# Retention's value and gate projection, and half of its query and key projection in layer two, as three products of parts

## The reference

```
mod = silu(c) @ w_ada[l] + b_ada[l]                 # shift, scale and gate, six times 1024
h = x * (1 + sc_m) + sh_m
(aq, ak, av, iq, ik, iw, rq, rk, rv, rg, mq, mk, mv, mo, mi, mf) = split(h @ w_in[l])   # 1024 x 3916
o_a = attention(rope(aq), rope(ak), av), the 64 best keys chosen by an index of iq, ik, iw
o_b = head_norm(retention(rope(rq), rope(rk), rv)) * silu(rg)
o_c = head_norm(sigmoid(mo) * mlstm(silu(conv(mq, mk)), mv, mi, mf))
x = layer_norm(ALPHA * x + (1 + g_m) * (concat(o_a, o_b, o_c) @ w_out[l]))
h = x * (1 + sc_f) + sh_f
x = layer_norm(ALPHA * x + (1 + g_f) * experts(h))   # 16 experts, 2 of them weighted per token
```

## Time and profile before

| | us |
|---|---|
| median of 3 runs | 1697.02 |
| lowest and highest of them | 1693.13, 1697.38 |
| the profiled execution's own time | 1697.81 |
| its span, first to last instruction | 1696.0 |
| TensorE, VectorE, ScalarE busy | 1634.5, 1082.3, 716.0 |

### The profile page before, as it was taken

How to read it: one execution, slowest core, us unless ns; L and a number is a source line. 1 busy time by engine, 2 the same in 40 slices (tenths; PEclk the granted TensorE clock), 3 DMA queues, 4 the chain that set the end, 5 groups by cost and what they waited for, 6 DMA issues and landing times.

```text
span 1696.0 us, 19169 instructions
## 1 busy us (share of the span) xinstructions
PE 1634.5 (96%) x7463; PEld 1244.0 (73%) x7463; DVE 1082.3 (64%) x1684; ACT 716.0 (42%) x1105; POOL 0.2 (0%) x4
## 2 busy tenths in 40 slices
PE   6999999999999999999999989899999998999998
PEld 5465568888885655688888878778887887788885
DVE  8678587776656765884545567864546767754445
ACT  1133343433421333433434346653436756643445
POOL 0000000000000000000000000000000000000000
PEclk9998999999999999999999999899999998999999
DMA  9856356877764633556555652146556451444641
GB/s 353 296 182 242 122 186 223 316 254 273 248 230 161 229 110 108 187 198 220 177 187 185 217 167 99 49 149 204 169 200 222 145 187 50 149 149 164 208 170 41
DMA packets 218538, 314.98 MB, mean 186 GB/s; under 512 B 22468, under 2 KB 147788, under 8 KB 218320
## 3 DMA queue, kind: packets, MB, share of 16 engines
q1 hardware_dynamic: 217760, 313.63, 53.6%
q10 hardware_dynamic: 688, 0.13, 0.0%
HBM read 312.70 MB, written 1.05 MB: 185 GB/s over the span
## 4 chain that ended last, share of the span: by engine, by line
PE 85%; DVE 10%; ACT 2%; issue 1%; DMA 1%; SPq 0%; DVEq 0%; ACTq 0%
PE psum L598 18%; PE psum L599 18%; PE psum L600 18%; PE psum L534 8%; PE psum L1008 3%; DVE tmp L1336 2%; PE psum L605 2%; DVE gring_parts L1333 1%; PE psum L1206 1%; PE psum L651 1%; PE psum L517 1%; PE psum L574 1%; PE psum L575 1%; DVE arena L1336 1%; PE psum L1182 1%
## 5 line engine op out<-in xcount | busy, mean ns | idle before, releaser
L600 PE MATMUL psum<-arena_parts,hT_parts 128*128 128x512 f32 x896 | 353.0, 394 | 0.0
L1333 DVE TENSOR_TENSOR gring_parts<-gring,arena_parts 128x2048 fp32r<-128x2048 f32 (+1 forms) x125 | 278.9, 2271 | 50.6 <-ACT arena_parts L2356 50.0
L2356 ACT ACTIVATE arena_parts<-gring 128x2048 fp32r<-128x2048 f32 (+1 forms) x125 | 231.3, 1904 | 0.4
L1333 DVE TENSOR_TENSOR arena_parts<-psum,ex_parts 128x256 fp32r<-128x256 f32 x106 | 44.5, 420 | 281.1 <-ACT ex_parts L2356 280.9
L2356 ACT ACTIVATE ex_parts<-psum 128x256 fp32r<-128x256 f32 x106 | 40.5, 382 | 394.2 <-PE psum L651 394.2
L598 PE MATMUL psum<-arena_parts,o_cat_parts 128*128 128x512 f32 x512 | 203.8, 398 | 0.0
L599 PE MATMUL psum<-gring_parts,o_cat_parts 128*128 128x512 f32 x512 | 202.3, 395 | 0.0
L600 PEld LDWEIGHTS psum<-arena_parts,hT_parts 128*128 128x128 f32 x896 | 168.5, 188 | 39.6
L534 PE MATMUL psum<-gring,hT 128*128 128x512 f32 x384 | 176.1, 609 | 2.5 <-DMA gring<-in_w_in 1.8
L598 PE MATMUL psum<-arena_parts,ex_parts 128*128 128x512 f32 x424 | 177.3, 418 | 0.3 <-DVE arena_parts L1333 0.3
L599 PE MATMUL psum<-gring_parts,arena_parts 128*128 128x512 f32 x432 | 170.3, 394 | 0.0
(11 more groups left out here) (268 smaller groups left out, 2386.5 us busy)
## 6 DMA issues: line engine op xcount, KB each, us to landing
gring<-in_w_ffn_in SPq DMA_DIRECT2D x44, 1024.0 KB, 8.8
gring<-in_w_ada SPq DMA_DIRECT2D x20, 2048.0 KB, 9.8
gring<-in_w_in SPq DMA_DIRECT2D x16, 2048.0 KB, 12.4
gring<-in_w_gate SPq DMA_DIRECT2D x32, 1024.0 KB, 7.4
gring<-in_w_up SPq DMA_DIRECT2D x32, 1024.0 KB, 9.8
dring<-in_w_down SPq DMA_DIRECT2D x32, 1024.0 KB, 5.0
dring<-in_w_ffn_out SPq DMA_DIRECT2D x22, 1024.0 KB, 5.0
gring<-in_w_out SPq DMA_DIRECT2D x8, 2048.0 KB, 8.7
```

The costliest lines, as they stand in the source:

```text
L600: return nc.tensor.matmul(ps, lo, w, start=False, stop=stop)
L1333: return nc.vector.tensor_tensor(o, a, b, op)
L2356: return nc.scalar.activation(o, a, ACT.Copy)
```

## The change

Where in_parts lists a range of k tiles of a chunk, these k tiles become products of parts: in layer one k tiles 0 to 3 and 6, 7 of rvg; in layer two 0 to 3 of rqk and all of rvg. The rounded weights get places that are free at that time: rows, tmp, the upper half of o_cat and parts of the arena. The rounded input (in_hi) and its rest (in_lo) lie in the two slots of dring. ScalarE makes the rounded parts (input_rounded, projection_rounded), VectorE the rests (input_rest, projection_rest). In layer one all this work is at s = 5 on ScalarE and at s = 7 on VectorE. In layer two the input's parts come ahead of the rotations of idx, rqk's behind att_exp(1) and att_in(1), rvg's at s = 5 and s = 7. The row loads move behind the loads of the second expert's gate and up weights, gu1. (blocks, queries and keys, pT_blocks and ex_blocks name places; not all are used.)

```diff
@@ -260,7 +260,7 @@
         cshared = sb("cshared", [P, C_SHARED])
         cblock = sb("cblock", [P, C1_W])
         crows = sb("crows", [NR, NR, P])
-        rows = sb("rows", [P, 2, D])
+        rows, rows_parts = sb_parts("rows", [P, 2, D])
         gb = sb("gb", [P, D])
         ones = sb("ones", [P, SEQ])
         pcol = sb("pcol", [P, 2 * P])
@@ -276,7 +276,7 @@
         hidT = ex_parts[:, 2, :].rearrange("p (t f n) -> p t f n", t=TT, f=FE // P)
         prm = ex[:, 1, 0:2 * P].rearrange("p (a n) -> p a n", a=2)
         small = sb("small", [P, SMALL])
-        tmp = sb("tmp", [P, 2, N])
+        tmp, tmp_parts = sb_parts("tmp", [P, 2, N])
         arena, arena_parts = sb_parts("arena", [P, ARENA])
         ident = cshared[:, 0:P]
         scoresT = tmp[0:NE, 0, 0:SEQ]
@@ -403,6 +403,7 @@
 
         roped = buf(3, N)
         idxT, aqT, akT, rrT = buf(3, SEQ), buf(4, SEQ), buf(4, SEQ), buf(4, SEQ)
+        at_rows = used[0] - SEQ * 4
         av, rvg = buf(TT, N), buf(TT, N)
         rv, rg = rvg[:, :, 0:256], rvg[:, :, 256:512]
         qkT, mo = buf(4, SEQ), buf(TT, 256)
@@ -410,6 +411,21 @@
         score = buf(SEQ)
         sm, pT = buf(2, N), buf(2, N)
         tail = used[0]
+
+        def blocks(at, n):
+
+            return arena_parts[:, at:at + n * N].rearrange("p (k n) -> p k n", n=N)
+
+        in_hi = dring_rest[:, 0].rearrange("p t (k n) -> p t k n", n=P)
+        in_lo = dring_rest[:, 1].rearrange("p t (k n) -> p (t k) n", n=SEQ)
+        first_half, upper = [a.rearrange("p t (k n) -> p (t k) n", n=N) for a in (rows_parts, o_cat_parts)]
+        queries, keys = blocks(at_rows, 8), upper
+        pT_blocks, ex_blocks, heads = blocks(tail - 2 * N, 2), ex_parts[:, 0:2, :], o_cat_parts[:, :, N:D]
+        in_parts = {
+            (0, "rvg"): [(0, 4, first_half), (6, 8, heads)],
+            (1, "rqk"): [(0, 2, blocks(at_rows, 2)), (2, 4, blocks(at_rows + 4 * N, 2))],
+            (1, "rvg"): [(0, 4, first_half), (4, 6, tmp_parts[:, :, :]), (6, 8, heads)],
+        }
         cin, mv = buf(4, SEQ + CONV - 1), buf(TT, NR, HD + 1)
         acc = tmp
 
@@ -533,6 +549,20 @@
             for k in ks:
                 last = nc.tensor.matmul(ps[:, 0:n], hT[:, k, t * P:(t + 1) * P], w[:, k, 0:n],
                                         start=k == 0, stop=k == KT - 1)
+            return last
+
+        def token_parts(ps, l, t, name, ks=range(KT)):
+
+            part_of = {k: (k0, a[:, k - k0, :]) for k0, k1, a in in_parts.get((l, name), ()) for k in range(k0, k1)}
+            n = slice(t * P, (t + 1) * P)
+            for k in ks:
+                if k in part_of:
+                    k0, w = part_of[k]
+                    if t == 0 and k == k0:
+                        pe.wait_ge(vector_done, V.at(T, ("in lo", name, k0)))
+                    last = split_product(ps, in_hi[:, t, k, :], in_lo[:, k, n], w, g_rest(T.stage, name)[:, k, 0:N], k == 0, k == KT - 1)
+                else:
+                    last = nc.tensor.matmul(ps, hT[:, k, n], gslot(T.stage, name)[:, k, 0:N], start=k == 0, stop=k == KT - 1)
             return last
 
         def wait_weights(name, q):
@@ -773,7 +803,7 @@
                 if name == "idx":
                     last = product_as_modulated(ps, t, gslot(stage, name), N_IDX)
                 else:
-                    last = token_product(ps, t, gslot(stage, name), N)
+                    last = token_parts(ps, l, t, name)
                 last.then_inc(tensor_done, T.step((name, t)))
 
             def half_in_proj(name, t, q):
@@ -782,7 +812,7 @@
                     if t == 0:
                         pe.wait_ge(G.sem(stage, name), G.level(stage, name))
                     take((name, t), V if name == "rqk" else A, 6 if (name, t) == ("rqk", 1) else 5)
-                last = token_product(bank(T, (name, t)), t, gslot(stage, name), N, range(4 * q, 4 * q + 4))
+                last = token_parts(bank(T, (name, t)), l, t, name, range(4 * q, 4 * q + 4))
                 if q:
                     last.then_inc(tensor_done, T.step((name, t)))
 
@@ -1645,6 +1675,21 @@
                     normed("in", t)
                 modulated("xT", "hT", 1, scale, shift)
 
+            def input_rest():
+
+                for t in range(TT):
+                    dve.wait_ge(scalar_done, A.at(V, ("in hi", t)))
+                    n = slice(t * P, (t + 1) * P)
+                    for half in range(2):
+                        k = slice(4 * half, 4 * half + 4)
+                        tt(in_lo[:, k, n], hT[:, k, n], in_hi[:, t, k, :], ALU.subtract).then_inc(vector_done, V.step())
+
+            def projection_rest(name):
+
+                for k0, k1, w in in_parts[l, name]:
+                    dve.wait_ge(scalar_done, A.at(V, ("in hi", name, k0)))
+                    tt(g_rest(stage, name)[:, k0:k1, 0:N], gslot(stage, name)[:, k0:k1, 0:N], w, ALU.subtract).then_inc(vector_done, V.step(("in lo", name, k0)))
+
             slots = {}
 
             def rope_chunk(name, t, nh):
@@ -1768,6 +1813,8 @@
                 dve.wait_ge(vector_done, V.now())
 
 
+            if l:
+                input_rest()
             for t in range(TT):
                 if l == 0:
                     rotation_tables(t)
@@ -1785,6 +1832,8 @@
             top_k(1)
             att_in(0)
             att_in(1)
+            if l:
+                projection_rest("rqk")
             for s in range(len(ATT)):
                 if s + 2 < len(ATT):
                     att_in(s + 2)
@@ -1820,6 +1869,9 @@
                         tt(wr_parts[:, :], wr[:, :], wr_hi_parts[:, :], ALU.subtract).then_inc(vector_done, V.step())
                         dve.wait_ge(vector_done, V.now())
                 if s == 7:
+                    if l == 0:
+                        input_rest()
+                    projection_rest("rvg")
                     rope_chunk("rqk", 1, 2 * NR)
                     columns_of(9)
                     if l == 0:
@@ -2465,6 +2517,22 @@
                     root_of("in", rstd[:, t:t + 1], t)
                     modulated_T("xT", "hT", t, *folded["mix"])
 
+            def input_rounded():
+
+                for t in range(TT):
+                    act.wait_ge(vector_done, V.at(A, ("hT", t, 0)))
+                    if l:
+                        act.wait_ge(tensor_done, T.of(FIRST[l - 1], ("dn1", NE - 1)))
+                        act.sem_inc(waited)
+                    act.wait_ge(scalar_done, A.now())
+                    copy(in_hi[:, t, :, :], hT[:, :, t * P:(t + 1) * P]).then_inc(scalar_done, A.step(("in hi", t)))
+
+            def projection_rounded(name, *free):
+
+                act.wait_ge(G.sem(stage, name), G.level(stage, name))
+                for k0, k1, w in in_parts[l, name]:
+                    copy(w, gslot(stage, name)[:, k0:k1, 0:N]).then_inc(scalar_done, A.step(("in hi", name, k0)))
+
             def row_T(name, dst, blocks, t):
                 act.wait_ge(tensor_done, T.at(A, (name, "T", t)))
                 ps = bank(A, (name, "T", t))
@@ -2476,6 +2544,8 @@
                 for t in range(TT):
                     row_T(name, dst, blocks, t)
 
+            if l:
+                input_rounded()
             rows_T("idx", idxT, 3)
 
             def relu(t):
@@ -2546,6 +2616,8 @@
             act.wait_ge(scalar_done, A.now())
             att_exp(0)
             att_exp(1)
+            if l:
+                projection_rounded("rqk")
             copied_mqk(1)
             for s in range(len(ATT)):
                 att_probs_T(s)
@@ -2562,6 +2634,14 @@
                         act.wait_ge(tables_loaded, 16 * TABLES)
                         act.wait_ge(vector_done, V.of("start", "wr_pad"))
                         copy(wr_hi_parts[:, :], wr[:, :]).then_inc(scalar_done, A.step("wr"))
+                if s == 5:
+                    if l == 0:
+                        input_rounded()
+                    else:
+                        act.wait_ge(vector_done, V.at(A, ("affine", "in", 1)))
+                        act.wait_ge(tensor_done, T.at(A, ("sum", "ada5")))
+                        act.sem_inc(waited)
+                    projection_rounded("rvg")
                 if s == 6:
                     act.wait_ge(vector_done, V.at(A, "conv"))
                     activate(qkT, qkT, ACT.Silu).then_inc(scalar_done, A.step("conv"))
@@ -2968,17 +3048,16 @@
                             sp.wait_ge(vector_done, V.at(S, ("read", ("out", 1, h))))
                         sp.sem_inc(waited)
                     load_gate_bias(l, 4)
-                if name == "wo1":
-                    if l:
-                        sp.wait_ge(vector_done, V.at(S, ("affine", "in", 1)))
+
+            def expert(name, e):
+                return by_row(ins[name][l:l + 1, e:e + 1].rearrange("a b c d -> (a b c) d"))
+
+            for e in range(NE):
+                load_halves(stage, f"gu{e}", expert("w_gate", e), expert("w_up", e))
+                if e == 1:
```

(7 more changed lines are left out.)

4 lines of the change are left out of this document (2 added, 2 removed).

## The result

| | median | from .. to | executions |
|---|---|---|---|
| before | 1697.84 us | 1693.02 .. 1698.49 | 9 |
| changed | 1702.45 us | 1699.03 .. 1706.63 | 9 |

The ratio is 1.0031, with a 95% interval of [1.002, 1.0041]: slower by 0.31%, about 5 us. The change was forecast at 1698.8. The time lies inside the range (1692.8 to 1703.0), near its upper end; it is just past 1702.1, where the forecast began to say slower, with a chance of 0.14. The profiled execution of the changed kernel took 1706.61 us (span 1704.8), one of its slowest; its mean granted clock was 0.979, against 0.984 before.

The account below looks back on a forecast made before the run. TensorE, at work for 96% of the span, was taken as the bound. Layer one +1.5, layer two -1.4 and clock +1.7 gave +1.8 on the profiled 1697.81, so 1699.6, or 1698.8 us on the median; range 1692.8 to 1703.0.

Parts of the forecast that it names:

- the clock: Behind the new gap ahead of rvg in layer one, one stretch at 1.2 GHz was counted, costing 1.66 us.
- The second rival: Slower by the clock in both layers: three 1.2 GHz stretches, +5.1 in sum, 1702.1 us; chance 0.15.
- Layer one, VectorE: Six subtractions ahead of the rotation take 6.27 us, only 2.72 of it in idle time; TensorE waits 3.5 (3.2 to 3.9).
- The sum of layer one: Layer one's wait for VectorE less the gain of shorter products: 3.5 - 1.98 = +1.5 us.
- Layer one, ScalarE: The copies behind att_exp(7) take 5.10 us in all and are hidden, with 0.2 to spare.
- Layer two, start: Two copies and four subtractions ahead of the rotations of idx cost 0; were they not hidden, at most 3.6.
- Layer two, mvo: Two copies ahead of the copy of mqk's second block hold up mvo: +0.6 us, bounds 0.4 and 0.7.
- Layer two, the lost gains: rqk's saving of 1.32 and that of rvg's first half end in waits for the Silu and the values.
- The halves: A half_in_proj call with all four k tiles as products of parts saves 0.66 us, one with two changed 0.33.
- The sum without the clock: Both layers' changes with no lower clock behind the new gap: +0.1 us.
- One rival's sum: No gain on TensorE, from equally slow products or late rvg weights: +6 us, 1703; chance 0.02.
- the 1.98 of layer one: Gain of layer one's four halves of rvg as products of parts: 0.66, 0.33, 0.66 and 0.33 us.

Follow-up runs that it names:

- the second trace: The changed kernel executed again with no edit: 1702.44 us, ratio 1.0027 to the kernel before.
- the moved loads: The kernel before with only the two row loads of the layer norm moved behind gu1: 1697.21 us, ratio 0.9995.
- layer two alone: The changed kernel with products of parts, copies and subtractions only in layer two, layer one as before: 1700.39 us, ratio 1.0002 to before.
- layer one filled: The changed kernel with five idle matmuls ahead of rvg in layer one only: 1701.7 us, ratio 1.002 to before.
- room and rqk: Parts for k tiles 4 to 7 of rvg in layer one, rvg and rqk in layer two: 1697.09 us, ratio 0.9993 to before.
- room: The changed kernel with parts only for k tiles 4 to 7 of rvg in layer one, and rvg in layer two: 1692.55 us, ratio 0.997 to before.
- layer one alone: The changed kernel with products of parts, copies and subtractions only in layer one, layer two as before: 1698.83 us, ratio 1.0003 to before.
- the gap alone: The kernel before with row loads moved and six unread VectorE subtractions of the same sizes in layer one, no parts: 1704.81 us, ratio 1.0033.
- layer two filled: The changed kernel with two idle matmuls ahead of mLSTM's first scores in layer two only: 1701.63 us, ratio 1.0016 to before.

## Why the prediction was wrong

**The step that failed is the clock:** "This gap is longer than those, so I count one such stretch", at 1.66. Both the number and the price were too low. Two stretches come in both traces of the changed kernel: behind the gap of layer one, 5.24 - 2.78 = 2.5, and behind the wait for the Silu (634 to 640), 6.22 - 3.70 = 2.5 on rqk alone. Together they are 5.0 where the sum has 1.7, and over the executions the clock's figure is 5.5 more than before, some of it in the gap itself. That is the miss: 1702.4 against 1698.8. The first profile has two more stretches. Whether the one from 172.75 belongs to the change is open: it is missing from the second trace, but both kernels with one gap filled have it (granted clock 0.83 and 0.80 from 170 to 180). The one at 650 can't be put down to the change: a stretch like it stands between 636 and 652 in the profile of each of the twelve experiments, in that of the moved loads too; only the profiled execution of the kernel before went without it.

The second rival, "slower, by the clock in both layers", described the mechanism with a wait of 1.3 more, and gave 1702.1; it was given 0.15. That its number fits so well is partly luck: it counts three stretches at 1.66 where there are two at 2.5. It was held down by one row, the window of the earlier trace rows with 2 us of gaps at a clock of 1.00. One gap without a slow stretch says that the stretch is not certain; it doesn't say that it is unlikely. Two of the three windows there showed the opposite, and behind the wait for the Silu a slow stretch came in all five profiles that have rqk as parts and nothing in that gap (the changed kernel twice, layer two alone, layer one filled, room and rqk). The Trainium skill's TensorE: Matmul & The Clock Gate, section HAM oscillation — how this bites in real kernels, has the engine throttled again at each wait of a loop and not once; its waits are longer (about 3 to 5 us). The trace agrees that each new gap has to be counted, with 0.50 behind two of them, one of them of 1.47 us.

**Layer one, VectorE.** Forecast: 6.27 of work, 3.5 late. The six took 5.75. The gap was put at 4.3 (160.9 to 165.2) and was 5.15, from 159.0 to 164.15, because the changed kernel ran half a microsecond ahead there (156.03 for 156.51) and the half of rqk ahead of the gap was not slow this time (3.70 for 5.06). So rvg started 2.5 later than in the earlier trace rows, and not 3.5. The forecast took the whole 2.72 as room for the new work, but this idle time ends when rqk does: with rqk at the full clock it would have been about 1.4, and rvg would have started near 160.3 (estimates from the 5.06 and 3.70), with the same small gap (0.94 in room, with rqk at 3.70). In the three traces that have the subtractions, or as many, behind a slow rqk of 6.0 to 6.5 (layer one alone, the gap alone, layer two filled) rvg started at 164.5 to 164.9; in the two without them (layer two alone, loads moved) at 163.0 to 163.1. So the delay is about 1.4 to 1.9 with a slow rqk, and about 3.9 with a quick one (164.15 against the estimate of 160.3); the 3.5 lies between the two. The sum of layer one was off by this too, in a direction that the draw decides.

**Layer one, ScalarE.** The copies took 5.15 (2.21, 1.90, 1.04) from 144.24 on, for 5.10 from 144.63; hidden, as forecast.

**Layer two, start.** Hidden as forecast: VectorE had 3.39 idle ahead of the rotation of aq, for 4.75 in the earlier trace rows.

**Layer two, mvo.** Forecast +0.6 for ScalarE's two copies ahead of that of mqk. The ladder has 5.60 at mvo against 5.47 ahead of it: +0.13. The bounds, 0.4 and 0.7, were both too high. ScalarE came to its two copies at 593.86, 0.4 earlier than 588.76 + 5.47, and the copies held it for 1.9, not 2.12.

**Layer two, the lost gains.** The wait for the Silu grew by 0.77, and 0.26 of waiting came for ScalarE's copy of pair six; 1.03 where 1.3 was forecast. The 0.74 ahead of the values came about as forecast (0.7). In the comparison of room with and without rqk the gain without the clock's figure lies between -0.5 and +0.1 us. What the forecast didn't say in its main line is what those two waits do: a gain that ends in a wait is not worth 0 but less.

**The halves.** 2.97 from the first start of a half to the next group, for 3.59: 0.62 saved where 0.66 was forecast.

**The sum without the clock.** Forecast +0.1; by the clock's figure -1.1 in the second series. In the first the clocks of the kernel before are not known; against those of a later series it is -0.6. As the figure also takes off time at the lower clock in which TensorE only waited, it makes the change look better than it is by up to about 1 us; the terms that are arithmetic on rows were right in sum within about a microsecond, though the 3.5 and the 0.6 were each off. One rival's sum, "+1.5 + 0.6 + 1.98 x 2 = +6", gives back the 1.98 of layer one twice and leaves out the clock's 1.66; the two slips nearly cancel (5.7).

**Open.** Why the clock falls at other places (172.75, 650), several microseconds after a gap and with TensorE at work all the time, is not settled. In room it falls with waits of only 0.70 and 0.74 ahead of it (636 to 640, 0.57), with the moved loads at 640 without any new wait. Why a half of rqk in layer one is slow in ten of the fourteen profiles and quick in four isn't settled either; that draw alone moves what the subtractions cost. Not tried: room with the first half of rvg in layer two plain, which would take away the 0.74. Nor do the runs tell what each of the two gaps is worth by itself: singly they give 2, together 4.4.

## What to carry to other kernels

On a kernel whose TensorE is 96% busy, ask of each edit first whether it makes TensorE stand, because a new gap is paid once as the wait and again in the clock behind it: the gap alone cost 6.1 us, and 2.4 with idle products in it. A product that is made faster ahead of a wait on another engine is better left slow, or the saved time filled with idle products: rqk in parts cost 4 us. And put the work that prepares faster products into the idle time that the helping engine really has; two thirds of the k tiles in the right place (room, 24 of 36, -5 us) beat all of them where two groups opened waits (+5 us). Take more than one trace of the kernel before, too: idle time and slow stretches in a single one can be a draw.

## What was not expected of the hardware

A stretch at 1.2 GHz ahead of a wait costs nothing where another engine's own work ends the wait (6.03 instead of 3.7 for rqk in layer one alone, and rvg starts 0.35 later than in the changed kernel). Where that engine waits for the slow product itself, the stretch costs its full length: without the subtractions rvg started at 159.37 behind a half of rqk of 3.70 (room), at 161.66 behind 5.06 (before) and at 163.03 behind 6.33 (loads moved), each time after a gap of 0.8 to 0.9. Waits of 1.46 and 1.47 us, in a stretch that is otherwise full, had eight records behind them at 5.61 to 6.22 in five profiles out of five. With 0.70 or 0.71 in that place they took 3.70 in six profiles out of seven; the seventh is the gap alone:

```profile
632.34 0.69 PE L955 MATMUL psum<-ex,crows 4*128 4x256 f32 x2 [0.70 <-ACT arena L2404]
...
633.81 5.40 PE L562 MATMUL psum<-gring,hT 128*128 128x512 f32 x8
```

So in these profiles the slow stretch comes more often behind the longer wait, and the length alone doesn't decide it. Seven idle products (4.51 + 1.88 us of work that is thrown away) made a kernel 4.3 ± 1.9 us faster. And the spread from execution to execution, 7.6 us in one kernel, follows the mean granted clock (correlation -0.9): which stretches are slow differs from one trace of a kernel to the next, and one profile shows one draw. The Trainium skill's TensorE: Matmul & The Clock Gate, section What's actually happening, says that the number of matmuls at the lower level at a kernel's start varies from run to run of the same kernel; the spread of the mean granted clock here, 0.979 to 0.984 in nine executions, agrees that the share at the lower level varies.
